# A decoder step's last stage: three of five running-sum additions move from VectorE to GpSimd

## The chip, the cores and the metric

One Trainium2 chip; the kernel is one program on one of its cores. The metric is the device time of one execution in microseconds, as the median of several runs. Durations and starts of single instructions come from one profiled execution, whose times are counted from the start of its span (its first to its last instruction).

## The reference

The kernel computes one inference step of a decoder layer for 512 prompt tokens and 32 sample tokens (8 sequences of 4), with a model width of 1024: modulated RMSNorm, one input projection, windowed attention with three dilations and a short gated convolution, an output projection with a gated residual, and then a mixture of experts with one shared expert:

```python
    x = x + g1 * (jnp.concatenate([attn, conv_out], axis=-1) @ w_o)
    h2 = _rmsnorm(x, norm2_g) * (1 + sc2) + sh2
    x = x + g2 * _moe(h2, w_router, b_router, w_gate_e, w_up_e, w_down_e,
                      w_gate_s, w_up_s, w_down_s)
```

`_moe` sends each token to 8 of 64 experts, sums their weighted results and adds the shared expert's result. Everything is float32. Only the last line, x + g2 * (routed + shared), is touched by the change, and of it only the way in which the routed part is put together.

## The kernel before

The 544 tokens stand in five tiles of up to 128 tokens on the partitions and 1024 columns. Tiles 0 to 3 are the prompt (128 tokens each), tile 4 holds the 32 sample tokens. All stages go through them in `ORDER = [4, 0, 1, 2, 3]`, so j = 0 is the small tile.

The program is written engine by engine, with semaphores for every dependency. SyncE (SP in the profile) issues the weight loads, GpSimd (POOL) the gathers and scatters of the expert stage, TensorE the matmuls, ScalarE and VectorE what stands between.

In the expert stage a loop runs over groups of experts, three tiles of gathered tokens in each round. GpSimd gathers token rows out of `h2_d` in DRAM by a list of indices in SBUF (`gather`, line 771) and scatters each expert's result rows back, adding them up in DRAM (`scatter`, line 776). So that two scatters can be under way at once there are two running sums, `y_d` and `z_d`; a token's routed result is the sum of the two. VectorE makes the next round's one-hot comparisons (`one_hot`, line 1928, two inputs in SBUF) at the head of each round.

Behind the loop GpSimd waits until all scatters and gathers have landed and raises `s_all` to 1 (line 831). SP waits for that and then loads, tile by tile in `ORDER`, the tile's part of `y_d` into `yf[tt]` (line 645) and of `z_d` into `zf[tt]` (line 646); both raise `s_yf[tt]`, by 16 each. `yf` and `zf` are ten buffers of their own in SBUF, one pair for each tile, so no load waits for another tile.

Meanwhile TensorE multiplies out the shared expert (line 1547), and VectorE multiplies that by the gate `g2` (line 2029, one input in PSUM) and adds it to the residual `x_t` (line 2031). Behind these ten half tiles VectorE runs the last loop, three operations for each tile on all 1024 columns, every input and output in SBUF:

```python
            for j, tt in enumerate(ORDER):
                n, s = nt(tt), int(tt == SAMPLE)
                eng.wait_ge(s_yf[tt], 32)
                link(eng.tensor_tensor(yf[tt][0:n, :], yf[tt][0:n, :], zf[tt][0:n, :], ALU.add))
                link(eng.tensor_tensor(yf[tt][0:n, :], yf[tt][0:n, :], g2[s][0:n, :], ALU.mult))
                eng.tensor_tensor(yf[tt][0:n, :], yf[tt][0:n, :], x_t[0:n, tt, :], ALU.add).then_inc(s_fin, 1)
```

These are lines 2032 to 2037. `link` makes VectorE wait for the operation's own end, because the next one reads its result. The third operation raises `s_fin`; SP, which has issued all loads by then, waits for `s_fin` to reach j + 1 and writes the tile to the output (line 649). The program ends when the five writes have landed. GpSimd has nothing to do after line 831.

Of the kernel before, what the change touches and what calls it, by code (L numbers as in the profile page):

```python
# [20 lines left out]
ALU = mybir.AluOpType  # L21
# [15 lines left out]
ORDER = [4, 0, 1, 2, 3]  # L37
# [38 lines left out]


ROLES = 4
QUART = NE // ROLES
CAPS = (160, 96, 64, 64)  # L80
UNIT = 64
ITERS = 2 * QUART
FAR = 1024.0
# [31 lines left out]
def constants():  # L115
    c = np.zeros((P, CSTW), np.float32)

    def put(name, a):
        o, w = CST[name]
        c[:, o:o + w] = a  # L120
# [17 lines left out]
    put("place", np.broadcast_to(np.arange(CAPS[0]) - FAR, (P, CAPS[0])))  # L138
    put("unit", np.broadcast_to((ROLES * np.arange(QUART)[None, :] + np.arange(ROLES)[:, None]).reshape(-1), (P, NE)))
    s = np.zeros((P, 16), np.float32)  # L140
# [122 lines left out]
def build(nc, a, out):  # L263
# [21 lines left out]
    with ExitStack() as ctx:  # L285
# [8 lines left out]
        def at(off, *dims, parts=P):  # L294
            n = int(np.prod(dims))
            v = mem[0:parts, off:off + n]
            if len(dims) == 2:
                v = v.rearrange("p (a b) -> p a b", a=dims[0])
            elif len(dims) == 3:
                v = v.rearrange("p (a b c) -> p a b c", a=dims[0], b=dims[1])  # L300
            return v
# [4 lines left out]
        def sem(name):  # L306
            return ctx.enter_context(nc.semaphore(name))
# [53 lines left out]
        def const(name, parts=P, w=None):  # L361
# [44 lines left out]
        e_cmp, e_ge, e_late = r_mr[0:NE, 0:NE], r_sel[0:NE, 0:NE], r_ma  # L406
        pos = at(m_vr + 6 * RW, TILES, ROLES * ITERS)
        rT = at(m_vr + 8 * RW, TILES * P, parts=NE)
# [4 lines left out]
            at(m_r + 4 * i, 1, parts=NE) for i in range(10))  # L413
        e_small = at(m_r + 40, QUART, parts=NE)

# [10 lines left out]
        yf = [at(m_ring + D * i, D) for i in range(TILES)]  # L426
        zf = [at(m_smp + D * i, D) for i in range(TILES)]
# [65 lines left out]
        s_lrow, s_all, s_yf, s_fin, s_yout = sem("s_lrow"), sem("s_all"), [sem(f"s_yf{i}") for i in range(TILES)], sem("s_fin"), sem("s_yout")  # L493
# [35 lines left out]
        def nt(j):  # L529
            return NS if j == SAMPLE else P  # L530
# [23 lines left out]
        def _(eng):  # L554
# [43 lines left out]
            def expert(c, i):  # L598
                at_ = bass.ds(ITERS * c + i, 1) if not isinstance(i, int) else slice(ITERS * c, ITERS * c + 1)
                return eng.value_load(meta[0:1, at_], min_val=0, max_val=NE - 1)  # L600

            def load_gu(c, e):
                for q, name in ((0, "w_gate_e"), (1, "w_up_e")):
                    eng.dma_start(wgu[c][:, q], a[name][0, bass.ds(e, 1)].rearrange("e (p k) f -> p (e k) f", p=P)  # L604
                                  ).then_inc(s_wgu[c], 16)
# [5 lines left out]
            eng.wait_ge(s_meta, 1)  # L611
            first = [expert(c, 0) for c in range(ROLES)]
            load_gu(0, first[0])
# [11 lines left out]
            eng.wait_ge(s_meta, 2)  # L625
            groups = eng.value_load(meta[0:1, P:P + 1], min_val=QUART, max_val=ITERS - 2)
            with eng.Fori(1, groups) as i:
                own = [expert(c, i) for c in range(ROLES)]
                eng.wait_ge(s_gu, 3 * i - 1)
# [26 lines left out]
        def _(eng):  # L656
# [96 lines left out]
            for to, done in ((y_d, s_sca), (z_d, s_scb)):  # L753
                for r0 in range(0, TR, P):
                    n = min(P, TR - r0)
# [33 lines left out]
            eng.wait_ge(s_meta, 2)  # L789
            groups = eng.value_load(meta[0:1, P:P + 1], min_val=QUART, max_val=ITERS - 2)  # L790
            added, also, copied = (eng.alloc_register(n) for n in ("added", "also", "copied"))
# [37 lines left out]
            for t in range(ET):  # L829
                eng.wait_ge(s_ga[t], 16 * groups + 32)  # L830
            eng.nop().then_inc(s_all, 1)


        @block.scalar
        def _(eng):
# [204 lines left out]
            eng.wait_ge(s_meta, 2)  # L1040
            groups = eng.value_load(meta[0:1, P:P + 1], min_val=QUART, max_val=ITERS - 2)
            with eng.Fori(0, groups) as i:
# [515 lines left out]
        def _(eng):  # L1558
            links = [0]

            def link(ins):

                links[0] += 1
                ins.then_inc(s_link, 1)
                eng.wait_ge(s_link, links[0])
# [17 lines left out]
            for j, tt in enumerate(ORDER):  # L1583
                n = nt(tt)
# [52 lines left out]
            for c in range(8):  # L1637
                for j, tt in enumerate(ORDER if c < 6 else range(3)):
                    n = nt(tt)
# [156 lines left out]
            for o in range(3):  # L1796
                c0, w = sum(WO_W[:o]), WO_W[o]
                for j, tt in enumerate(ORDER):
                    u, n, s = 5 * o + j, nt(tt), int(tt == SAMPLE)
# [88 lines left out]
            eng.wait_ge(s_route, 3)  # L1888
            ids = meta[0:1, 0:P].rearrange("p (c h n) -> p c h n", c=ROLES, h=2)
            eng.tensor_copy(ids[:, :, 0, :], pb[7][NE:NE + 1, P:P + NE].rearrange("p (c n) -> p c n", c=ROLES)  # L1890
# [134 lines left out]
            for u in range(2 * TILES):  # L2025
                tt, cols = ORDER[u // 2], slice(512 * (u % 2), 512 * (u % 2) + 512)
                n, s = nt(tt), int(tt == SAMPLE)
# [4 lines left out]
            for j, tt in enumerate(ORDER):  # L2032
                n, s = nt(tt), int(tt == SAMPLE)
                eng.wait_ge(s_yf[tt], 32)
                link(eng.tensor_tensor(yf[tt][0:n, :], yf[tt][0:n, :], zf[tt][0:n, :], ALU.add))
                link(eng.tensor_tensor(yf[tt][0:n, :], yf[tt][0:n, :], g2[s][0:n, :], ALU.mult))
                eng.tensor_tensor(yf[tt][0:n, :], yf[tt][0:n, :], x_t[0:n, tt, :], ALU.add).then_inc(s_fin, 1)

# [23 lines left out]
```

## Time and profile before

| | |
|---|---|
| median of 3 runs | 1200.81 us (1199.27 to 1202.39) |
| the profiled execution | 1203.46 us, span 1201.6 us |
| VectorE (DVE) busy | 448.8 us, 37% of the span |
| GpSimd (POOL) busy | 266.7 us, 22% of the span |
| last signal of GpSimd (line 831) | at 1172.1 us |
| last loop of VectorE | from 1180.2 to 1198.5 us |

A row of the page's fifth part, or of a view by lines, names the line, the engine, the operation, what it writes and reads, and how many there were; then the busy time in us with the mean duration in ns of one, and the idle time ahead of them with what ended it. In the time line each row is a start and a duration in us. The chain of work that ended last is followed back from the last instruction, at each step to what released it.

### The profile page before, as it was taken

How to read it: one execution, taken by the hardware profiler on the slowest of the kernel's cores; microseconds unless marked ns; L12 is line 12 of the kernel's file. 1: busy time of each engine (PE TensorE's matmuls, PEld its weight loads, DVE VectorE, ACT ScalarE, POOL GpSimd, SP SyncE). 2: the span in 40 equal slices, each digit the busy share in tenths (PEclk: the TensorE clock that was granted, in tenths of full speed). 3: DMA queues.
4: the chain of work that ended last, by engine and by line, in shares of the span. 5: the costliest groups of instructions: out<-in, count | busy, mean ns of one | idle time of the engine just before them, and what ended most of it. 6: DMA issues, size and time to landing. Idle time of an engine off the chain costs nothing.

```text
span 1201.6 us, 16610 instructions
## 1 busy us (share of the span) xinstructions
PE 1090.0 (91%) x5866; PEld 539.1 (45%) x5866; DVE 448.8 (37%) x1005; ACT 205.2 (17%) x445; POOL 266.7 (22%) x282
## 2 busy tenths in 40 slices
PE   5999899998999969999998998998889889998992
PEld 3455455556776557544442433343334323332430
DVE  0445775405553367323230322232122303221248
ACT  4311110003342023011110111011111101110110
POOL 1011222102204100222322231323132222312230
PEclk9999999997999988999998998999999999898996
DMA  9888799944655951789999999999999999999955
GB/s 322 304 309 310 247 333 268 262 165 181 226 144 191 347 221 71 298 352 376 380 370 373 401 386 369 384 382 384 344 393 373 369 353 391 375 345 378 334 109 223
DMA packets 80885, 370.73 MB, mean 309 GB/s; under 512 B 12897, under 2 KB 27278, under 8 KB 52647
## 3 DMA queue, kind: packets, MB, share of 16 engines
q1 hardware_dynamic: 47088, 258.50, 54.3%
q0 software_dynamic: 26848, 81.95, 25.0%
q10 hardware_dynamic: 6916, 29.84, 6.9%
q8 instruction: 21, 0.34, 0.1%
q14 instruction: 12, 0.10, 0.0%
HBM read 342.62 MB, written 66.02 MB: 340 GB/s over the span
## 4 chain that ended last, share of the span: by engine, by line
PE 54%; DMA 34%; DVE 7%; issue 2%; SPq 1%; ACT 1%; POOL 0%; ACTq 0%; DVEq 0%; POOLq 0%
DMA mem<-in_w_up_e 33%; PE pb L1482 14%; PE pb L1188 10%; PE pb L1343 4%; PE pb L1192 4%; PE pb L1502 3%; PE pb L1076 2%; PE pb L1103 2%; PE pb L1321 2%; PE pb L1414 2%; PE pb L1262 2%; PE pb L1547 1%; SPq L604 1%; PE pb L1275 1%; DVE mem L1790 1%
## 5 line engine op out<-in xcount | busy, mean ns | idle before, releaser
L1482 PE MATMUL pb<-mem 128*32 128x512 f32 (+2 forms) x1792 | 360.2, 617 | 41.6 <-DMA mem<-in_w_up_e 41.6
L1482 PEld LDWEIGHTS pb<-mem 128*32 128x32 f32 (+2 forms) x1792 | 121.4, 134 | 266.8 <-issue 266.8
L1502 PE MATMUL pb<-mem 128*32 128x512 f32 (+2 forms) x896 | 177.5, 597 | 6.6 <-ACT mem L1050 6.6
L1991 DVE SCALAR_TENSOR_TENSOR mem<-pb,mem 128x256 f32<-128x256 f32 x48 | 32.7, 680 | 346.3 <-ACT mem L1046 276.8
L776 POOL DMA_INDIRECT y_d<-mem x48 | 69.8, 1453 | 308.9 <-DMA y_d<-mem 176.3
L1188 PE MATMUL pb<-mem 128*128 128x384 f32 x384 | 129.6, 492 | 0.0
L1076 PE MATMUL pb<-mem 128*128 128x128 f32 (+2 forms) x649 | 92.3, 285 | 29.9 <-DMA mem<-in_k_cst 10.4
L1076 PEld LDWEIGHTS pb<-mem 128*128 128x128 f32 (+2 forms) x649 | 74.5, 148 | 82.0 <-issue 50.8
L771 POOL DMA_INDIRECT mem<-h_d,mem x54 | 67.5, 1250 | 160.3 <-issue 132.9
L1502 PEld LDWEIGHTS pb<-mem 128*32 128x32 f32 (+2 forms) x896 | 57.0, 129 | 101.8 <-issue 101.8
L1188 PEld LDWEIGHTS pb<-mem 128*128 128x128 f32 x384 | 71.6, 191 | 57.5 <-issue 8.8
L1046 ACT ACTIVATE mem<-pb 128x256 f32<-128x256 f32 x48 | 18.4, 383 | 364.5 <-PE pb L1482 364.5
L1997 DVE COPY mem<-pb 128x512 f32<-128x512 f32 x48 | 33.2, 692 | 92.5 <-PE pb L1502 92.5
L1343 PE MATMUL pb<-mem 128*128 128x384 f32 (+1 forms) x192 | 55.9, 452 | 0.0
L776 POOL DMA_INDIRECT z_d<-mem x32 | 45.8, 1432 | 25.5 <-DVE mem L1997 11.2
L1343 PEld LDWEIGHTS pb<-mem 128*128 128x128 f32 x192 | 36.2, 190 | 19.7 <-issue 1.2
L1928 DVE TENSOR_TENSOR mem<-mem 128x320 bf16<-128x320 f32 (+3 forms) x90 | 43.7, 554 | 0.9 <-issue 0.9
L1055 ACT ACTIVATE mem<-pb 128x512 f32<-128x512 f32 x48 | 28.6, 595 | 87.6 <-DVE mem L2005 43.9
L1192 PE MATMUL pb<-mem 128*128 128x512 f32 x96 | 42.7, 597 | 0.0
L1621 DVE TENSOR_TENSOR mem<-mem 128x1024 f32<-128x1024 f32 (+1 forms) x24 | 29.3, 1219 | 26.3 <-DMA mem<-new_d 26.0
L1956 DVE COPY mem<-pb 128x512 f32<-128x512 f32 x51 | 35.3, 692 | 3.0 <-PE pb L1076 2.5
L712 POOL DMA_DIRECT2D mem<-in_cache_k_w x24 | 12.8, 535 | 102.2 <-DVE mem L1623 101.1
(263 smaller groups left out, 989.9 us busy)
## 6 DMA issues: line engine op xcount, KB each, us to landing
mem<-in_w_gate_e SPq DMA_DIRECT2D x64, 1024.0 KB, 16.9
mem<-in_w_up_e SPq DMA_DIRECT2D x64, 1024.0 KB, 24.9
mem<-in_w_down_e SPq DMA_DIRECT2D x64, 1024.0 KB, 24.0
mem<-in_w_ada SPq DMA_DIRECT2D x24, 1024.0 KB, 11.9
mem<-in_w_in SPq DMA_DIRECT2D x8, 1536.0 KB, 13.9
mem<-new_d POOLq DMA_DIRECT2D x16, 512.0 KB, 8.5
out<-in_cache_k_w ACTq DMA_DIRECT2D x8, 1020.0 KB, 7.5
out<-in_cache_v_w ACTq DMA_DIRECT2D x8, 1020.0 KB, 20.9
```

The costliest lines, as they stand in the source:

```text
L771: eng.indirect_dma_start(out=xg[t][:], out_offset=None, in_=h2_d, in_offset=bass.IndirectOffsetOnAxis(ap=ix[:, t:t + 1], axis=0), bounds_c ...
L776: eng.indirect_dma_start(out=to, out_offset=bass.IndirectOffsetOnAxis(ap=ixs[0:hi - lo, col:col + 1], axis=0), in_=yo[t][lo:hi, :], in_off ...
L1076: return eng.transpose(dst, src, ident[0:parts, 0:parts])
L1188: mm = eng.matmul(pb[z % 2][0:nt(tt), 0:PJ_W], lhsT=hT[:, k, tok(tt)], rhs=w[:, k, :], start=(k == 0), stop=(k == KD - 1))
L1192: eng.matmul(pb[z % 2][:, :], lhsT=w[:, k, P * j:P * (j + 1)], rhs=hT[:, k, 0:SEQ], start=(k == 0), stop=(k == KD - 1))
L1343: mm = eng.matmul(pb[u % 2][0:nt(tt), 0:WO_W[o]], lhsT=catT[:, k, tok(tt)], rhs=w[:, k, :], start=(k == 0), stop=(k == KD - 1))
L1482: mm = eng.matmul(pb[t % 2][lo:hi, :].rearrange("p (q f) -> p q f", q=2), lhsT=xT[t][:, k, lo:hi], rhs=wgu[c][:, :, k, :], start=(k == 0), ...
L1502: mm = eng.matmul(pb[2 + half][lo:hi, :], lhsT=he[t][:, f, lo:hi], rhs=wdn[c][:, f, 512 * half:512 * half + 512], start=(f == 0), stop=(f ...
L1928: last = eng.tensor_tensor(oneh[:, :, lo:lo + n], pos[:, :, at_].to_broadcast([P, TILES, n]), const("place")[:, p0:p0 + n].unsqueeze(1).to ...
L1956: eng.tensor_copy(xT[t][:, 4:8, :], pb[XB[t] + 1][:, :].rearrange("p (k n) -> p k n", k=4)).then_inc(s_xd, 1)
L1991: eng.scalar_tensor_tensor(out=hh[t].rearrange("p (k f) -> p f k", k=2), in0=pairs(pb[t % 2][:, FE:2 * FE]), scalar=gcol[t], in1=pairs(sge ...
L1997: eng.tensor_copy(yo[t][:, 512:D], pb[3][:, :]).then_inc(s_yd, 1)
```

## The change

GpSimd gets, behind line 831, three additions: for j = 2, 3 and 4 it waits for the two loads of the tile and adds `zf` to `yf` in place, raising `s_all` to 2, 3 and 4. VectorE no longer makes these three additions; ahead of its product for such a tile it waits for `s_all` to reach the tile's count. For j = 0 and 1 nothing is changed, nor are the product, the second addition, the loads and the writes.

```diff
+POOL_SUMS = (2, 3, 4)
...
             eng.nop().then_inc(s_all, 1)
+            for j in POOL_SUMS:
+                tt = ORDER[j]
+                eng.wait_ge(s_yf[tt], 32)
+                eng.tensor_tensor(yf[tt][0:nt(tt), :], yf[tt][0:nt(tt), :], zf[tt][0:nt(tt), :], ALU.add).then_inc(s_all, 1)
...
                 eng.wait_ge(s_yf[tt], 32)
-                link(eng.tensor_tensor(yf[tt][0:n, :], yf[tt][0:n, :], zf[tt][0:n, :], ALU.add))
+                if j in POOL_SUMS:
+                    eng.wait_ge(s_all, POOL_SUMS.index(j) + 2)
+                else:
+                    link(eng.tensor_tensor(yf[tt][0:n, :], yf[tt][0:n, :], zf[tt][0:n, :], ALU.add))
                 link(eng.tensor_tensor(yf[tt][0:n, :], yf[tt][0:n, :], g2[s][0:n, :], ALU.mult))
```

## Rows read from the trace of the kernel before

**Rows 1.** The page, part 4: the chain that ended last, by engine.

```profile
PE 54%; DMA 34%; DVE 7%; issue 2%; SPq 1%; ACT 1%; POOL 0%; ACTq 0%; DVEq 0%; POOLq 0%
```

**Rows 2.** Instructions of line 831: duration ns min/median/max, first and last start us.

```profile
L831 POOLq EVENT_SEMAPHORE  x1: 43/43/43, 1172.1 to 1172.1; - x1
```

**Rows 3.** The chain in order of time, tail: start us, us, what.

```profile
1179.48 0.70 DVE mem L2031
1180.19 0.02 issue
1180.21 1.23 DVE mem L2035
1181.43 0.02 issue
1181.46 1.22 DVE mem L2036
...
1197.31 1.23 DVE mem L2037
```

**Rows 4.** The time line of the tail: start us, us, engine, line, operation.

```profile
1166.76 1.43 POOL L776 DMA_INDIRECT z_d<-mem  x1 [0.30 <-issue]
...
1187.49 1.22 DVE L2035 TENSOR_TENSOR mem<-mem 128x1024 f32<-128x1024 f32 x1
1188.74 1.23 DVE L2036 TENSOR_TENSOR mem<-mem 128x1024 f32<-128x1024 f32 x1
1190.00 1.22 DVE L2037 TENSOR_TENSOR mem<-mem 128x1024 f32<-128x1024 f32 x1
...
1193.65 1.23 DVE L2037 TENSOR_TENSOR mem<-mem 128x1024 f32<-128x1024 f32 x1
...
1198.56 0.33 SPq L649 DMA_DIRECT2D out<-mem  x1
```

**Rows 5.** Transfers by issue: what, queue, count, KB each, median us to landing.

```profile
out<-mem SPq DMA_DIRECT2D x4, 512.0 KB, 2.6
```

**Rows 6.** Loads of j = 2, 3, 4, issue by issue: start, us to landing.

```profile
1173.92 0.43 SPq L645 DMA_DIRECT2D mem<-y_d  x1
DMA to landing us min/median/max: 6.1/6.1/6.1
1174.39 0.44 SPq L646 DMA_DIRECT2D mem<-z_d  x1
DMA to landing us min/median/max: 7.0/7.0/7.0
1174.88 0.49 SPq L645 DMA_DIRECT2D mem<-y_d  x1
DMA to landing us min/median/max: 7.7/7.7/7.7
1175.41 0.49 SPq L646 DMA_DIRECT2D mem<-z_d  x1
DMA to landing us min/median/max: 8.5/8.5/8.5
1175.94 0.59 SPq L645 DMA_DIRECT2D mem<-y_d  x1
DMA to landing us min/median/max: 9.2/9.2/9.2
1176.58 0.85 SPq L646 DMA_DIRECT2D mem<-z_d  x1
DMA to landing us min/median/max: 9.8/9.8/9.8
```

**Rows 7.** GpSimd by line and shape: the memsets.

```profile
L767 POOL MEMSET mem<- 128x1088 f32 x3 | 2.9, 1002 | 35.4 <-DMA h_d<-mem 35.4
...
L657 POOL MEMSET mem<- 33x12 f32 x1 | 0.1, 101 | 0.3 <-POOLq L2050 0.3
```

**Rows 8.** The time line: gathers of GpSimd beside comparisons of VectorE.

```profile
519.23 0.99 POOL L771 DMA_INDIRECT mem<-h_d,mem  x1 [19.01 <-DVE mem L1944]
519.32 2.44 DVE L1928 TENSOR_TENSOR mem<-mem 128x640 bf16<-128x640 f32 x5 [0.85 <-issue]
...
752.47 0.82 DVE L1928 TENSOR_TENSOR mem<-mem 128x640 bf16<-128x640 f32 x1
752.54 1.68 POOL L771 DMA_INDIRECT mem<-h_d,mem  x1 [11.43 <-issue]
756.10 0.99 POOL L771 DMA_INDIRECT mem<-h_d,mem  x1 [0.30 <-issue]
...
957.84 2.43 DVE L1928 TENSOR_TENSOR mem<-mem 128x640 bf16<-128x640 f32 x5
958.07 1.51 POOL L771 DMA_INDIRECT mem<-h_d,mem  x1 [7.68 <-issue]
...
1080.38 0.81 DVE L1928 TENSOR_TENSOR mem<-mem 128x640 bf16<-128x640 f32 x1
1080.54 1.58 POOL L771 DMA_INDIRECT mem<-h_d,mem  x1 [5.53 <-issue]
```

**Rows 9.** Busy time by stretch of 2 us: PE, PEld, DVE, ACT, POOL, PEclk, DMA, GB/s.

```profile
1182.00:1184.00 2.00, 0.00 (x0) 0.00 (x0) 1.97 (x3) 0.00 (x0) 0.00 (x0) 0.76 1.03 420
```

## The prediction

> **What bounds the kernel now.** I read the time and the span first, then the chain of work that ended last, then the last 40 us alone. The whole run is TensorE and weight transfers: on the page the chain is 54% PE, 34% DMA and 7% DVE [rows 1]. The change touches none of that; it sits behind line 831, where GpSimd signals that the last scatter has landed, at 1172.1 us of a span of 1201.6 us [rows 2]. So only the last 30 us can move. There the chain has one owner [rows 3]: from 1180.21 us VectorE runs 15 additions and products one behind the other, three for each tile (L2035 sum of the two running sums, L2036 times the gate, L2037 plus the residual), and between them stand only pieces of 0.02 us called issue. No piece of it is a wait for a transfer. The last one ends at 1197.31 + 1.23 = 1198.54 us, the last write is issued at 1198.56 [rows 4] and lands 2.6 us later [rows 5]; some 0.4 us more belong to the end of the program. GpSimd has no row at all after its last scatter at 1166.76 us, 1.43 us long [rows 4], so it is free.
>
> The profiled execution took 1203.46 us, of which 1201.6 is the span; the median of the runs is 1200.81 us, that is 2.65 us less. I work out differences within the span and add them to the median. The measurement can tell about 0.3%, here 3.6 us, from no change.
>
> **What the change removes.** For the tiles j = 2, 3, 4 (tokens 128 to 511) VectorE loses L2035. From the start of L2035 to the start of L2036 behind it is 1188.74 - 1187.49 = 1.25 us [rows 4]; the three groups are alike, each operation 1.22 to 1.23 us [rows 4]. Removed from VectorE's chain: 3 x 1.25 = 3.75 us.
>
> **What it adds, and when that can start.** GpSimd gets three additions of 128x1024 f32, each behind the loads of its tile. The loads of j = 2 are issued at 1173.92 and 1174.39 and land 6.1 and 7.0 us later: 1180.0 and 1181.4. Those of j = 3 land at 1174.88 + 7.7 = 1182.6 and 1175.41 + 8.5 = 1183.9, those of j = 4 at 1175.94 + 9.2 = 1185.1 and 1176.58 + 9.8 = 1186.4 [rows 6]. So GpSimd's first addition can begin at 1181.4, when VectorE has just started its second operation of tile j = 0. None can lie before VectorE's chain, and all of them must lie beside it. VectorE needs the sums, in the new order, at 1187.49 (j = 2), and, with operations of 1.22 to 1.25 us, at about 1190.0 and 1192.4.
>
> **The price of one addition on GpSimd.** No row shows GpSimd doing arithmetic on two tensors. The nearest are its memsets: 128x1088 in 1002 ns, and 33x12 in 101 ns [rows 7]. Taken as a fixed part and a rate, that is 0.10 us and (1002 - 101) / (1088 - 12) = 0.84 ns for each element of one stream. An addition has two streams in and one out. If all three passed side by side it would be 0.10 + 0.86 = 0.96 us; two passes (the inputs through one reading port) give 1.82 us, three passes with no overlap 2.68 us. The ends are far apart and no row is nearer to one of them; an addition must read twice, so the lower end is unlikely, and I take the middle of the two others, 2.25 us as an estimate, and keep 0.96 to 2.68 for the range. The Trainium skill (GPSIMD Engine Reference, section 3.1, Elementwise — side-by-side cycle accounting) gives 4497 ns for an fp32 addition of 2048 elements; half of it would be 2.25 us by its figure, no run here shows it yet, and the sum below would be the same by it.
>
> **Whether it lies beside VectorE's work.** This decides the sign. The trace of before has a case of the two engines meeting: at the head of each round of the expert loop VectorE runs L1928, comparisons with both inputs in SBUF, while GpSimd issues the gathers L771, which begin by reading their indices out of SBUF. A gather that meets nothing takes 0.99 us [rows 8]. One that starts 0.07 us behind the start of a 0.82 us comparison takes 1.68 us, one that starts 0.16 us behind takes 1.58, one 0.23 us behind 1.51 [rows 8]. Start plus lengthening gives 0.07 + 0.69 = 0.76, 0.16 + 0.59 = 0.75, 0.23 + 0.52 = 0.75: each was held to the same point, 0.75 us into the comparison and so nearly its end, and got in ahead of the next comparison. So a VectorE operation with two SBUF inputs keeps GpSimd's reads out for nearly its whole length. All 12 operations that VectorE keeps in the tail are of that kind. The other direction, VectorE held by a GpSimd instruction that came first, is not shown: a gather reads a handful of numbers. A gather that started 0.09 us ahead of five comparisons left them at 2.44 us, against 2.43 us elsewhere [rows 8]. By symmetry I take it that a long read of GpSimd's holds VectorE too. The Trainium skill says just that (SBUF — State Buffer, section Who interferes with whom): a VectorE instruction with two SBUF inputs contends with a GpSimd instruction that reads SBUF, and whichever starts first keeps the other out until it is done. This rule speaks against the change; the trace agrees with one half of it by the 0.75 us, and no run here shows the other half.
>
> **The sum.** If the port serves one of them at a time, the order does not matter as long as one of them is always at work: VectorE's 12 operations and GpSimd's 3 stand end to end from 1180.21 us. Removed 3.75, added 3 x 2.25 = 6.75, net +3.0 us. From this I take off what needs no port, GpSimd's fixed 0.10 us for each, 3 x 0.10 = 0.3, since it can pass while VectorE works: +2.7 us. Behind that nothing changes: the writes land 2.6 us after their issue [rows 5] and come every 3.66 us now (L2037 starts at 1190.00 and 1193.65 [rows 4]), so they never touch each other, and do not at 2.5 us spacing with 1.3 us of transfer each either (512 KB at the 420 GB/s of the stretch 1182 to 1184 [rows 9]). The prediction is 1200.81 + 2.7 = 1203.5 us. With two passes it is 3 x (1.82 - 0.10 - 1.25) = +1.4, 1202.2 us; with three passes 3 x (2.68 - 0.10 - 1.25) = +4.0, 1204.8 us.
>
> The added waits: VectorE's wait on s_all in L2036's place has behind it only the rest of this loop, and SP's write of that tile waits for VectorE anyway. GpSimd's own waits on s_yf have nothing behind them but the additions. SP's queue is as before.
>
> **The rivals.**
> 1. **No contention.** The gathers may be held by something that a plain addition doesn't use, and the two run side by side. Then from 1181.4 three additions of 2.25 us end at 1183.7, 1186.2 (its loads land at 1183.9) and 1188.7 (loads at 1186.4), each ahead of the 1187.49, 1190.0 and 1192.4 at which VectorE asks. All 3.75 us are gained: 1197.1 us, 0.31% faster. For it: VectorE was never seen held. Against it: the 0.75 us above.
> 2. **Shared in finer grain.** The port passes single reads of both in turn, so that GpSimd's additions fit partly into what VectorE's operations leave open. An addition then costs VectorE between the one-stream price and two passes: 3 x (0.96 - 1.25) = -0.9 to +1.4 us, 1199.9 to 1202.2 us.
> 3. **Slower.** The port is held whole, and the addition or its handover is dearer: place, VectorE's operations from 1181.4 us on, each pushed by one GpSimd addition. It becomes a loss over 0.3% from the point where an addition keeps the port for 1.25 + 3.6 / 3 = 2.45 us. Three passes reach 2.58 us without the fixed part; with the fixed part not hidden and a handover of 0.1 us for each (an estimate: five of the pieces of 0.02 us in the chain [rows 3]) it is 3 x (2.78 - 1.25) = +4.6 us. So 1204.4 to 1205.4 us. For it: no row shows GpSimd reading a wide tensor, and nothing rules out three passes. Against it: 2.25 us is under the point.
>
> **How the numbers follow.** Serialised at 1202.2 to 1204.4 us: 0.50, and with it the prediction of 1203.5. Slower: 0.27. Finer grain: 0.10. No contention: 0.13, of which 0.10 would measure as faster by over 0.3% (1197.1 is right at the bound of 1197.2) and 0.03 as the same. So faster 0.10, within 0.3% 0.50 + 0.10 + 0.03 = 0.63, slower 0.27. No contention has to be in the range to leave less than 2 in 10 out together with the ends of the others: 1197.0 to 1206.0 us.
>
> **What would show it.** In the profile of the changed kernel three GpSimd rows at the added line, the first starting at 1181 to 1183 us, tell the price of an addition. If the port is held, VectorE's rows in the tail are no longer 1.22 us: two or three of the operations beside a GpSimd addition last 2 us or more, or stand behind an idle gap of that length, while the operations after GpSimd's last addition are 1.22 us again; the last L2037 ends near 1201.2 us. If there is no contention every row of VectorE stays 1.22 us and the last ends near 1194.8. If GpSimd is kept out by back-to-back operations until VectorE stops to wait, its first addition starts at 1187.5 us and VectorE's idle time stands ahead of L2036, with the same end. What would make the prediction wrong: an addition far from 2.25 us, VectorE's operations not held by GpSimd, or the first GpSimd addition paying a start that no row of before shows.

## The result and the profile after

The changed kernel takes 1204.63 us (median of 20 runs, 1201.46 to 1207.43) against 1202.34 us before (20 runs, among them the three of the prediction); the ratio is 1.0019, with a 95% interval of 1.001 to 1.0028. So it is 1.2 to 3.4 us slower, some 2.3 us. The profiled execution took 1204.61 us with a span of 1202.8 us.

The time line of the tail (start us, us, engine, line, operation; L2044 is the sum, L2045 the product, L2046 the residual, L837 the new addition, L647 the first load) shows what happened. This time line and those below show only the rows of the engines that are spoken of.

```profile
1170.71 0.34 SPq L647 DMA_DIRECT2D mem<-y_d  x1
...
1178.78 1.21 DVE L2044 TENSOR_TENSOR mem<-mem 32x1024 f32<-32x1024 f32 x1
1179.99 2.33 POOL L837 TENSOR_TENSOR mem<-mem 128x1024 f32<-128x1024 f32 x1 [13.28 <-DMA mem<-z_d]
1180.03 3.37 DVE L2045 TENSOR_TENSOR mem<-mem 32x1024 f32<-32x1024 f32 x1
1182.54 3.06 POOL L837 TENSOR_TENSOR mem<-mem 128x1024 f32<-128x1024 f32 x1 [0.22 <-DMA mem<-z_d]
1183.43 3.24 DVE L2046 TENSOR_TENSOR mem<-mem 32x1024 f32<-32x1024 f32 x1
1186.61 3.35 DVE L2044 TENSOR_TENSOR mem<-mem 128x1024 f32<-128x1024 f32 x1
1189.99 1.23 DVE L2045 TENSOR_TENSOR mem<-mem 128x1024 f32<-128x1024 f32 x1
1191.25 1.22 DVE L2046 TENSOR_TENSOR mem<-mem 128x1024 f32<-128x1024 f32 x1
1192.39 1.22 DVE L2045 TENSOR_TENSOR mem<-mem 128x1024 f32<-128x1024 f32 x1
...
1198.43 1.23 DVE L2046 TENSOR_TENSOR mem<-mem 128x1024 f32<-128x1024 f32 x1
1199.69 0.33 SPq L651 DMA_DIRECT2D out<-mem  x1
```

Read it in pairs. GpSimd's first addition starts at 1179.99, when its loads have just landed, 0.04 us ahead of VectorE's product, and lasts 2.33 us. The product, 1.21 us in the kernel before, lasts 3.37. It ends at 1183.40, and only then does the second addition, issued at 1182.54, get on: its row is 3.06 us long, and VectorE's next row, 3.24 us, contains most of it. The third pair is the same, with 3.35 us in VectorE's row. From 1189.99 on, when GpSimd is done, every row of VectorE is 1.22 or 1.23 us again. The three long rows are over their usual length by 3.37 - 1.21 = 2.16, 3.24 - 1.21 = 2.03 and 3.35 - 1.22 = 2.13 us, 6.32 us in all. VectorE lost three sums of 1.25 us, 3.75 us. The difference is +2.57 us.

The tail as a whole shows the same. In the kernel before the first load is issued here:

```profile
1172.13 0.34 SPq L645 DMA_DIRECT2D mem<-y_d  x1
```

From there to the end of VectorE's last operation [rows 3] the kernel before took 1198.54 - 1172.13 = 26.41 us, the changed one 1199.66 - 1170.71 = 28.95 us: +2.54 us. The span grew by 1.2 us only, because in this execution the first load was issued 1.42 us earlier. Ahead of line 831 nothing was changed, and the runs of one kernel lie up to 6 or 7 us apart, so I put that down to chance; that is not shown.

The chain of work that ended last shows the same three operations, and no wait for a sum between them (start us, us, what):

```profile
1180.03 3.38 DVE mem L2045
1183.41 0.02 issue
1183.43 3.24 DVE mem L2046
1186.68 3.29 DVE mem L2044
```

By the view of waits VectorE waits for no sum either, and it looks busy: the page has it at 451.6 us against 448.8 before, with three instructions fewer. A held operation is counted as a busy one.

### The profile page after: what moved, and what is told of

Its sections match the earlier page's. It is cut to its first block, busy times and chain, and to the rows that moved or that the text cites. A ratio compares the mean times of both kernels' runs of the same rounds, so it can differ in the third digit from the quotient of the medians.

```text
span 1202.8 us, 16615 instructions
## 1 busy us (share of the span) xinstructions
PE 1091.1 (91%) x5866; PEld 539.8 (45%) x5866; DVE 451.6 (38%) x1002; ACT 205.2 (17%) x445; POOL 275.0 (23%) x285
## 4 chain that ended last, share of the span: by engine, by line
PE 55%; DMA 34%; DVE 6%; issue 2%; SPq 1%; ACT 1%; POOL 0%; ACTq 0%; DVEq 0%; POOLq 0%
DMA mem<-in_w_up_e 33%; PE pb L1488 14%; PE pb L1194 10%; PE pb L1349 4%; PE pb L1198 3%; PE pb L1508 3%; PE pb L1082 2%; PE pb L1109 2%; PE pb L1327 2%; PE pb L1420 2%; PE pb L1268 2%; PE pb L1553 1%; SPq L606 1%; PE pb L1281 1%; DVE mem L1796 1%
## 5 line engine op out<-in xcount | busy, mean ns | idle before, releaser
L1061 ACT ACTIVATE mem<-pb 128x512 f32<-128x512 f32 x48 | 28.6, 595 | 87.7 <-DVE mem L2011 44.0
L1041 ACT ACTIVATE mem<-pb 128x512 f32<-128x512 f32 x51 | 30.5, 597 | 26.5 <-PE pb L1082 26.5
```

## The experiments

The theory, as in the prediction: VectorE and GpSimd read SBUF in part through the same port; whichever operation came first keeps it to its end, if VectorE's has two inputs in SBUF and GpSimd's reads SBUF. In the runs called loose the kernel is the one before, and GpSimd does work beside it on buffers that are no longer used (the `xg` tiles of the gathers), so that nothing depends on it. Each loose kernel was run once, in the profile, and whole times of one kernel lie several us apart. So the loop's length and single rows are compared there, and not the whole time.

**Additions that nobody waits for.**

```diff
             eng.nop().then_inc(s_all, 1)
+            for k, tt in enumerate(ORDER[2:]):
+                eng.wait_ge(s_yf[tt], 32)
+                eng.wait_ge(s_all, k + 1)
+                eng.tensor_tensor(xg[2][:, 0:D], xg[0][:, 0:D], xg[1][:, 0:D], ALU.add).then_inc(s_all, 1)
```

> The kernel before with three additions of 128x1024 on GpSimd, on buffers that nobody else uses any more, released by the loads of tiles j = 2, 3, 4 as in the change; VectorE keeps its 15 operations and waits for none of them (the extra sums are used nowhere). Theory (the port is held whole by whichever came first): three of VectorE's operations last about 1.22 + 2.1 = 3.3 us, and the last loop takes 18.3 + 3 x 2.1 = 24.7 us from the first start to the last end. Rival, the loss is the waiting of VectorE for a sum on another engine: nothing waits here, 18.3 us. Rival, single reads take turns: the additions grow past 2.33 us and more than three operations of VectorE grow, each by less than 1 us.

The time line of its tail (L2039, L2040, L2041 are VectorE's three operations):

```profile
1176.36 1.21 DVE L2039 TENSOR_TENSOR mem<-mem 32x1024 f32<-32x1024 f32 x1
1177.52 2.33 POOL L835 TENSOR_TENSOR mem<-mem 128x1024 f32<-128x1024 f32 x1 [13.15 <-DMA mem<-z_d]
1177.61 3.31 DVE L2040 TENSOR_TENSOR mem<-mem 32x1024 f32<-32x1024 f32 x1
1180.07 6.34 POOL L835 TENSOR_TENSOR mem<-mem 128x1024 f32<-128x1024 f32 x2 [0.22 <-DMA mem<-z_d]
1180.96 3.24 DVE L2041 TENSOR_TENSOR mem<-mem 32x1024 f32<-32x1024 f32 x1
1184.13 3.35 DVE L2039 TENSOR_TENSOR mem<-mem 128x1024 f32<-128x1024 f32 x1
...
1199.73 1.23 DVE L2041 TENSOR_TENSOR mem<-mem 128x1024 f32<-128x1024 f32 x1
```

The loop takes 1200.96 - 1176.36 = 24.60 us against 18.33 before and 24.7 expected. The three rows are long by 2.10, 2.03 and 2.13 us, nearly the same amounts as in the changed kernel. So the loss has nothing to do with VectorE waiting for GpSimd's sums: work without any dependency costs 6.27 us. That three operations carry all of it, and the others nothing, speaks against single reads that take turns.

**Writes in place of reads.** The line of the addition becomes `eng.memset(xg[2][:, 0:D], 0.0).then_inc(s_all, 1)`.

> As loose_adds, with three memsets of 128x1024 in place of the additions: GpSimd writes and reads nothing. Theory, in its form that the reads are what collides: VectorE's operations stay at 1.22 us, the last loop takes 18.3 us. Rival, any access of GpSimd to SBUF holds VectorE: three operations grow by the length of a memset, some 0.9 us, and the loop takes 21.0 to 21.2 us.

```profile
1180.38 0.95 POOL L835 MEMSET mem<- 128x1024 f32 x1 [12.82 <-DMA mem<-z_d]
1180.83 1.21 DVE L2040 TENSOR_TENSOR mem<-mem 32x1024 f32<-32x1024 f32 x1
...
1182.93 0.95 POOL L835 MEMSET mem<- 128x1024 f32 x1 [1.60 <-DMA mem<-z_d]
1183.22 1.21 DVE L2039 TENSOR_TENSOR mem<-mem 128x1024 f32<-128x1024 f32 x1
```

In the time line each of the three memsets lies beside operations of VectorE and takes 0.95 us, and no row of VectorE is longer for it; the loop takes 1197.91 - 1179.58 = 18.33 us, as before. These writes of GpSimd's cost VectorE nothing. What the additions have and the memsets don't is the reads.

**One stream read.** The line becomes `eng.tensor_copy(xg[2][:, 0:D], xg[0][:, 0:D]).then_inc(s_all, 1)`.

> As loose_adds, with three copies of 128x1024 in place of the additions: one stream read, one written. Theory: each copy holds VectorE for about its own length, so by an estimate of one stream at the memset's rate some 0.9 us each, and the loop takes about 21.1 us. Rival, only an operation with two inputs on GpSimd collides: 18.3 us. Rival, the price is one for each meeting, whatever is read: 24.7 us as with the additions.

```profile
1181.92 1.31 POOL L835 COPY mem<-mem 128x1024 f32<-128x1024 f32 x1 [12.81 <-DMA mem<-z_d]
1182.37 1.94 DVE L2040 TENSOR_TENSOR mem<-mem 32x1024 f32<-32x1024 f32 x1
1184.34 1.21 DVE L2041 TENSOR_TENSOR mem<-mem 32x1024 f32<-32x1024 f32 x1
1184.48 1.99 POOL L835 COPY mem<-mem 128x1024 f32<-128x1024 f32 x1 [1.24 <-DMA mem<-z_d]
1185.48 2.05 DVE L2039 TENSOR_TENSOR mem<-mem 128x1024 f32<-128x1024 f32 x1
```

The loop takes 1201.74 - 1181.12 = 20.62 us, 2.29 us more than before and a little under the expected 21.1: each copy holds one operation for 0.72 to 0.83 us. One input is enough to collide. The copy of 1184.48 also shows the other direction: issued 0.14 us into VectorE's operation of 1184.34, it waits for that and takes 1.99 us.

**Half the width.** The additions become 128x512: `eng.tensor_tensor(xg[2][:, 0:512], xg[0][:, 0:512], xg[1][:, 0:512], ALU.add)`.

> As loose_adds, with additions of 128x512. Theory: VectorE is held for as long as the addition reads, so about half of 2.1 us for each, and the loop takes 18.3 + 3 x 1.05 = 21.5 us. Rival, a fixed price for each meeting (a handover of the port): 24.7 us as with the whole additions.

```profile
1181.22 1.26 POOL L835 TENSOR_TENSOR mem<-mem 128x512 f32<-128x512 f32 x1 [13.22 <-DMA mem<-z_d]
1181.25 2.30 DVE L2040 TENSOR_TENSOR mem<-mem 32x1024 f32<-32x1024 f32 x1
```

The loop takes 1201.44 - 1180.00 = 21.44 us, 21.5 expected. The first hold is 2.30 - 1.21 = 1.09 us, half of 2.16, the other two are 1.06 and 0.94. So the hold goes with what GpSimd reads and is not a fixed price for a meeting. From 2.33 us for 1024 columns and 1.26 for 512 an addition of GpSimd costs, as an estimate from these two, (2.33 - 1.26) / 512 = 2.09 ns for each column and 0.19 us.

**A VectorE operation with an input in PSUM.** The loose additions are released earlier, by the shared expert's matmuls:

```diff
+            for k, u in enumerate((6, 7, 8)):
+                eng.wait_ge(s_sd_, u + 1)
+                eng.wait_ge(s_all, k + 1)
+                eng.tensor_tensor(xg[2][:, 0:D], xg[0][:, 0:D], xg[1][:, 0:D], ALU.add).then_inc(s_all, 1)
```

> The kernel before with the three loose additions of GpSimd (128x1024, on buffers nobody else uses; the extra sums are used nowhere) moved ahead of the last loop: each is released by the matmul that also releases VectorE's product of a half tile, which has one input in PSUM and one in SBUF, 0.69 us; behind it stands the addition to the residual with both inputs in SBUF, 0.69 us. Theory (only VectorE operations with two SBUF inputs collide): the product that runs beside the addition's start stays at 0.69 us, the addition to the residual behind it grows by the rest of the hold, 2.1 - 0.7 = 1.4 us, to about 2.1 us. The 15 operations of the last loop stay at 1.22 us and it takes 18.3 us. Rival, GpSimd's reads hold every VectorE operation that touches SBUF: the product itself grows to 2 us or more.

Its time line (L2033 reads PSUM and SBUF, L2035 reads SBUF twice):

```profile
1174.69 7.85 POOL L835 TENSOR_TENSOR mem<-mem 128x1024 f32<-128x1024 f32 x3 [5.42 <-PE pb L1551]
1174.71 0.69 DVE L2033 TENSOR_TENSOR mem<-pb,mem 128x512 f32<-128x512 f32 x1 [0.30 <-PE pb L1551]
1175.44 2.15 DVE L2035 TENSOR_TENSOR mem<-mem 128x512 f32<-128x512 f32 x1
1177.62 0.69 DVE L2033 TENSOR_TENSOR mem<-pb,mem 128x512 f32<-128x512 f32 x1
1178.35 2.00 DVE L2035 TENSOR_TENSOR mem<-mem 128x512 f32<-128x512 f32 x1
```

L2033 runs for its usual 0.69 us while an addition is under way, L2035 behind it takes 2.15 in place of 0.69. The last loop is 1202.90 - 1184.58 = 18.32 us. Both as expected: the operation with one input in SBUF and one in PSUM doesn't collide, the one with two in SBUF does. (An operation whose only input is in SBUF was not tried.)

**The other tiles.** `POOL_SUMS = (0, 1)` in the changed kernel: GpSimd adds where VectorE still has operations out of PSUM.

> The change with the tiles swapped: GpSimd adds the sums of j = 0 and 1, whose loads land some 3 and 6.5 us after the first load is issued, VectorE those of j = 2 to 4. Theory: part of each addition lies beside VectorE's products out of PSUM and beside idle stretches ahead of matmuls, of 0.3 us for each half tile, so less than 2.1 us of each is paid, and 2 x 1.25 = 2.5 us are saved: between 2 us less and 1.7 us more than before, a smaller loss than the change as made, or none. Rival, an addition always costs VectorE its 2.1 us: 2 x (2.1 - 1.25) = 1.7 us more than before.

The first of the two additions in the time line (L2035 reads PSUM and SBUF, L2037 reads SBUF twice):

```profile
1175.52 2.34 POOL L837 TENSOR_TENSOR mem<-mem 32x1024 f32<-32x1024 f32 x1 [6.89 <-DMA mem<-z_d]
1175.77 0.69 DVE L2035 TENSOR_TENSOR mem<-pb,mem 128x512 f32<-128x512 f32 x1 [0.30 <-PE pb L1553]
1176.49 1.92 DVE L2037 TENSOR_TENSOR mem<-mem 128x512 f32<-128x512 f32 x1
```

Measured: 1203.13 us, ratio to the kernel before 1.0007 (0.9993 to 1.002): no change that could be told. GpSimd's additions took 2.34 and 2.35 us, and the two operations that were held 1.92 and 1.99 us in place of 0.69, 2.53 us more in all, where 2 x 1.25 = 2.5 us are saved. The part of an addition that lies beside a PSUM operation is free, and that is enough to break even and no more. (The addition of the small tile, 32 partitions, took as long as one of 128.)

**The sums on TensorE.** If the port is the price, an engine that reads SBUF by another way should add for nothing. For every half tile TensorE multiplies both parts by the identity into the accumulator of the shared expert's result, and VectorE makes product and addition on that:

```diff
+                eng.matmul(pb[u % 8][0:n, :], lhsT=ident[0:n, 0:n], rhs=yf[tt][0:n, 512 * half:512 * half + 512],
+                           start=False, stop=False)
+                eng.matmul(pb[u % 8][0:n, :], lhsT=ident[0:n, 0:n], rhs=zf[tt][0:n, 512 * half:512 * half + 512],
+                           start=False, stop=True).then_inc(s_sd_, 1)
...
-            for j, tt in enumerate(ORDER):
-                n, s = nt(tt), int(tt == SAMPLE)
-                eng.wait_ge(s_yf[tt], 32)
...
```

> Neither engine adds the running sums: TensorE multiplies both loaded tiles by the identity into the accumulator that already holds the shared expert's result, and VectorE makes one product out of PSUM and one addition to the residual for each half tile, 20 operations of 0.69 us in all, where before it had these 20 and 15 of 1.22 us behind them. Theory (GpSimd's price is its port, and VectorE's chain is what ends the program): no operation of VectorE is held, the end is set by the last loads (they land 14 us after the first is issued), two matmul pairs and three or four operations of VectorE behind them; VectorE ends some 6 to 8 us earlier than before, 1194 to 1196 us in all. Rival, the tail is bound by the loads and the writes as well: a gain of 3 us or less. Rival, TensorE's clock falls while it waits for the loads and the pairs take 2.4 us for each half tile: ends 4 to 6 us earlier.

Measured: 1203.19 us, ratio to the kernel before 0.9999 (0.9986 to 1.0011), where 6 to 8 us less were expected. A miss. No operation of VectorE was held, but TensorE had become the chain. By stretches (us, PE, PEld, DVE, ACT, POOL busy, PEclk, DMA share, GB/s) and in the time line of the end:

```profile
1179.00:1183.00 4.00, 4.00 (x5) 1.51 (x5) 1.36 (x2) 0.00 (x0) 0.00 (x0) 0.50 1.01 408
1187.00:1200.00 13.00, 12.36 (x29) 5.13 (x27) 7.61 (x12) 0.00 (x0) 0.00 (x0) 1.00 0.30 121
```

```profile
1195.76 1.88 PE L1547 MATMUL pb<-mem 128*128 128x512 f32 x4
1195.96 0.69 DVE L2041 TENSOR_TENSOR mem<-pb,mem 128x512 f32<-128x512 f32 x1 [2.02 <-PE pb L1556]
```

Ten pairs of 1.72 us are 17 us, which I had counted for the last tile only; the last two half tiles of the shared expert, 1.72 us each, had slid to the end behind the banks they need; and the granted clock fell to 0.50, 1.2 GHz, where a pair takes 3.57 us (L1554 starts at 1179.52, its next at 1183.09). The wait for the first loads was only 0.56 us, up to 1175.03, and the clock was still 1.00 from 1176 to 1177 us. It was 0.78 from 1177 to 1178 and 0.50 from 1178 to 1184, and what TensorE did before it fell was that wait and the small tile's pairs, on 32 rows and 32 columns of the array. Which of the two brought it down no run separates.

**Half of it on TensorE.** So only the last two tiles' sums go to TensorE; VectorE keeps the first three, and all of the shared expert's matmuls stay ahead. For the last two tiles VectorE's product and addition out of PSUM now serve the shared and the routed part at once. So it loses all six operations of 1.22 us there, and not only the two sums. In one version six matmuls whose result is used nowhere keep TensorE at work until tile j = 3 lands:

```diff
+            eng.wait_ge(s_ysh, 3)
+            for k in range(6):
+                eng.matmul(pb[2][:, :], lhsT=hs[:, 0, tok(0)], rhs=wd[:, 0, 0:512], start=True, stop=True)
+            for u in range(6, 2 * TILES):
+                sums(u)
```

> The sums of the last two tiles (j = 3, 4) on TensorE, accumulated by the identity into the shared expert's accumulator; those of j = 0 to 2 on VectorE as before, which also evacuates the shared expert's first six half tiles as before. Six matmuls whose result is used nowhere keep TensorE busy between the shared expert's last matmul and the landing of tile j = 3. From the first load's issue to the last end of VectorE the kernel before took 26.4 us. Theory (TensorE reads SBUF past the port that VectorE and GpSimd quarrel over, and four half tiles of 1.72 us at full clock start at 11.8 us behind the first issue): TensorE ends at 18.7 us, VectorE 1.4 us later at about 20.1 us, so about 6 us less than before, 1196 us. Rival, VectorE is still the bound with 9 operations of 1.22 us and 8 of 0.69 us from about 3 us on: 19.9 us, the same. Rival, the clock falls all the same and a half tile takes 3.4 us: 26.9 us, no gain.

> As split_warm without the six filling matmuls, so TensorE has nothing to do for some 5 us ahead of the sums. If the granted clock falls to half in that pause, as it did in sums_on_pe (0.50 from 1179 to 1183 us, half tiles of 3.4 us and more), the first half tiles take 3.4 us in place of 1.72 and the end comes 3 to 7 us later than with the filling; if not, the two are alike.

With the filling: 1196.92 us, ratio to the kernel before 0.9948 (0.9932 to 0.9963). Without: 1199.06 us, 0.9968 (0.9956 to 0.998). Both beat the kernel before, where the changed kernel lost; it was not run beside them. With the filling the time line is

```profile
1183.92 1.22 DVE L2052 TENSOR_TENSOR mem<-mem 128x1024 f32<-128x1024 f32 x1
1185.06 0.68 DVE L2042 TENSOR_TENSOR mem<-pb,mem 128x512 f32<-128x512 f32 x1
...
1190.80 0.69 DVE L2044 TENSOR_TENSOR mem<-mem 128x512 f32<-128x512 f32 x1
```

VectorE goes from its last tile, the row of 1183.92, into TensorE's with no idle time ahead of it; ahead of the half tiles behind that it waits 0.17 to 0.30 us for TensorE. It ends 1191.49 - 1171.06 = 20.43 us behind the first load's issue, 20.1 expected, 26.41 before. TensorE's reads hold nothing of VectorE's here: the row of 1183.92 is 1.22 us long although TensorE reads tile j = 3 beside it, from 1182.90 on. The gain of 5.98 us in the tail goes with the six operations that VectorE no longer makes, 6 x 1.25 = 7.5 us, less the time that it now waits. Without the filling TensorE is idle for 5.34 us, and by stretches the clock is

```profile
1180.00:1182.00 2.00, 0.00 (x0) 0.00 (x0) 1.95 (x2) 0.00 (x0) 0.00 (x0) 0.76 1.04 422
1182.00:1184.00 2.00, 0.30 (x1) 0.30 (x2) 1.97 (x3) 0.00 (x0) 0.00 (x0) 0.50 1.03 401
1184.00:1186.00 2.00, 2.00 (x3) 0.88 (x3) 1.97 (x2) 0.00 (x0) 0.00 (x0) 0.50 1.02 379
1186.00:1188.00 2.00, 2.00 (x3) 0.68 (x2) 0.63 (x2) 0.00 (x0) 0.00 (x0) 0.53 0.90 367
1188.00:1190.00 2.00, 2.00 (x6) 0.95 (x5) 1.41 (x3) 0.00 (x0) 0.00 (x0) 1.00 0.21 86
```

so the first half tile pays the lower clock in full (3.58 us from 1183.70) and the second in part (2.01). In this execution the end comes 22.32 us behind the first issue, 1.9 us later than with the filling, less than the 3 to 7 expected: from the third half tile on the clock was back.

## Why the prediction was right

The sign and the size were right: +2.7 us forecast, +2.3 us measured in the runs and +2.54 in the tail of the profiled executions. The time, 1204.63 us, is 1.1 us above the 1203.5 forecast, and that is the base: the three runs that I added to had a median of 1200.81, the twenty that the result is compared with 1202.34, 1.53 us more, and the difference came out 0.4 us smaller. With that base the time lies just within the 1204.4 to 1205.4 us that I gave for the slower rival. What tells the two apart is the difference and the rows, not the time.

- **What bounds the tail.** Right. The changed chain is still VectorE's operations one behind the other, and the write behind the last is issued 0.03 us after it.
- **The removed part.** 3.75 us, as counted: VectorE's pairs of operations start 2.40 us apart (1189.99 and 1192.39 for L2045), where the triples started 3.65 us apart (1193.65 - 1190.00 [rows 4]; the prediction has 3.66 for it).
- **The price of an addition.** 2.25 us was the middle of two bounds from memsets; held by nothing, the addition takes 2.33 (the first L837 row). It is over the two passes (1.82) and under the three (2.68). No row before spoke for the middle, so that it came within 0.08 us is luck as far as the rows go, and near the lower bound the loss would have been +1.4 us. The estimate from the Trainium skill's figure (GPSIMD Engine Reference, section 3.1, Elementwise — side-by-side cycle accounting), half of 4497 ns, is 0.08 us short of what was measured.
- **The collision.** The step that carried the sign was inferred from gathers that were held to 0.75 us into a comparison [rows 8]. It holds in both directions, and loose_adds, loose_memsets, loose_copies and loose_early show what it depends on. What was only taken by symmetry, VectorE held by a GpSimd operation that came first, is seen at 1180.03: 3.37 us for 1.21. This is the rule of the Trainium skill (SBUF — State Buffer, section Who interferes with whom), the half that no row of before could show included: reads collide, writes don't, and the operation with one input in SBUF stays free. The runs show which operations hold each other; that a shared port does it is the Trainium skill's explanation in that section, which has the hold last for the whole instruction. Here each hold was 0.17 to 0.30 us shorter than the addition.
- **What needs no port.** I took off 0.10 us for each addition. The holds were 2.16, 2.03 and 2.13 us of 2.33, so 0.17 to 0.30 us of each lay beside VectorE's work. The term was under-sized by about half, and it is luck that the dearer addition makes up for part of it: 3 x 2.15 = 6.45 us forecast for the holds, 6.32 us measured.
- **The order of things.** I gave no order. GpSimd came first by 0.04 us and then the two alternated, one operation each, until GpSimd had no more to do. That the sum would be the same in another order, as the prediction said, is not shown. The end that it gave as a sign, 1201.2 us, came at 1199.66, which is 1201.08 with the tail's 1.42 us earlier start put back.
- **The rivals.** No contention would have left VectorE's rows at 1.22 us; three are 3.2 to 3.4. The finer grain would have spread the loss; loose_adds has it in three rows. The slower case needed a hold of 2.45 us; the largest is 2.16.

## What to carry to other kernels

An idle engine is not free help if it reads through a port of the busy one: ask of each pair of operations that would run side by side how many inputs each takes from SBUF, and look in the trace for a place where the two engines already meet. In these runs work put on GpSimd was free only as far as it lay beside VectorE operations with an input in PSUM, or only wrote. Here the relief paid when TensorE made the sums in an accumulator that it held anyway: that took from VectorE the sums and, for the same tiles, the separate product and residual addition. It paid for the last two tiles, whose sums TensorE had ready about when VectorE came to them, most with its clock kept up, and not for all five.

## What the runs showed that was not expected

- GpSimd's addition takes 2.35 us for 128x1024 and 2.34 us for 32x1024 in early_pair: between these two the number of partitions makes no difference.
- In the changed kernel and in loose_early the profile has two instructions called MODIFY_POOL_CONFIG of 11 ns each ahead of GpSimd's first addition, and no start price is seen behind them: in loose_early they stand at 1173.2 us, and the addition starts at 1174.69, with VectorE's product that the same matmul released at 1174.71.
- In sums_on_pe the granted clock fell to 0.50 although TensorE had waited only 0.56 us; between the wait and the fall it worked on the small tile, with 32 of its rows and columns.
- Each time the operation that had been waiting came next: the second addition, held since 1182.54, went ahead of VectorE's row of 1183.43, and the third one ahead of the row of 1186.61. So VectorE's back-to-back operations did not keep GpSimd out.
